# Experts' weights loaded in pairs of units, with the array laid out in order of use

## The chip, the cores and the metric

One core of a Trainium2 chip runs the whole kernel. The metric is the device time of one execution in microseconds, as the median of several runs. The profile is one further execution under the hardware profiler.

## The reference

One layer of a diffusion backbone over 1024 tokens of width 1024. A first part (modulated RMSNorm, one input projection, a long convolution and a neighbourhood attention, two branches merged by gates, an output projection) gives the residual stream `x`. The change concerns what follows, a mixture of experts with expert choice:

```python
def _ec_ffn(h, w_router, w_gate, w_up, w_down):
    cap = EC_CAPACITY * L // N_EXPERTS                        # 2 * 1024 / 16 = 128
    aff = jax.nn.softmax((h @ w_router).astype(jnp.float32), axis=-1)
    g, idx = lax.top_k(jnp.swapaxes(aff, 1, 2), cap)
...
    def expert(args):
        xe, wg, wu, wd = args
        return (jax.nn.silu(xe @ wg) * (xe @ wu)) @ wd
    y_e = lax.map(expert, (x_e, w_gate, w_up, w_down))
```

Each of 16 experts takes the 128 tokens with the highest affinity. Its three matrices are 1024 x 2816, 1024 x 2816 and 2816 x 1024 in float32. The results, weighted by the affinity, are added at the tokens' rows, and a gated residual and a last RMSNorm end the layer.

## The kernel before

The weights of all experts are arranged on the host (`units_laid_out`) as **units**: 128 partitions x 2048 floats, 1 MB, 8 KB per partition. An expert has 33 of them (`UNITS`): for each of six chunks `c` of the 2816 columns two units of gate and two of up, and for the chunk before it two of down; the last chunk is 256 wide and its gate and up share units ("both"). `STREAM` is the order in which units are used: expert by expert, except that the last unit of expert e, `CARRIED`, comes after the first two units of expert e+1. `PLACE` gives the place g of a unit in this order; there are N_ALL = 528.

The precision of a float32 product is had from three faster products: ACT copies a unit into a rounded high part `w_hi` (`split` on the scalar engine, L2702), DVE subtracts it from the raw unit for the low part `w_lo` (L2769), and PE multiplies high by high, low by high and high by low (L2657 for gate and up, L2647 for down): 12 matmuls of 512 columns for a unit. Ten units of expert 0 (`WHOLE`: places 0, 1, 4 to 7, 10 to 13) are not split; PE multiplies them as they are (L2623).

Three rings carry this. `raw` holds `RAW` = 8 units as they came; `w_hi` and `w_lo` hold `PARTS` = 6 each. SP loads unit g into slot g % 8 as soon as unit g-8 has been read for the last time, that is when its low part is ready, or when PE has used it if it is in `WHOLE`:

```python
for g in range(RAW, N_ALL):
    if g - RAW in WHOLE:
        sp.wait_ge(used, g - RAW + 1)
    else:
        sp.wait_ge(lo_ready, parts_until(g - RAW))
    sp.dma_start(raw[:, g % RAW], unit_source(a, g)).then_inc(raw_in[g % RAW], 16)
```

Each slot has its semaphore `raw_in[slot]`, which rises by 16 for each load. ACT's split of g waits for it and for `used` of g-6; DVE's for ACT's; PE waits for `lo_ready`. The first eight units are loaded one at a time by the stage before (`project_out`, L2028), while other transfers run.

The order on each engine is written out. ACT and DVE walk over g, split unit g and do what `STEPS` puts at g: silu of a gate chunk, the product with up (`moe_h`), the copy and low part of the transposed hidden chunk (`moe_ht_hi`, `moe_ht_lo`), the same for the tokens, the scaled output. In expert 0 DVE also finds the tokens of experts 1 to 15, in 16 rounds (`next_round`, L2779 to L2782) of which three come before the first unit and the others at g of `ROUNDS_AT` = 4, 5, 6, 7, 8, 10, 11, 12, 13, 14, 16, 17, 18. A down unit on PE waits for `h_parts`, which `moe_ht_lo` of its chunk raises: unit 8 for chunk 0, unit 14 for chunk 1. The low part of chunk 1 stands on DVE behind the split and the round of g = 17.

Of the kernel before, what the change touches and what calls it, by code (L numbers as in the profile page):

```python
# [1933 lines left out]
def project_out(nc, sems, a, keep, m_t, raw, raw_in, halves, gate_col, idx_col):  # L1934

    ident = keep["ident"]
    with ExitStack() as ctx:
# [56 lines left out]
        with nc.Block() as block:  # L1994

            @block.sync
            def _(sp):
                mod = a["mod_d"]
                x_t, acc_t, h2_t_d = (a[n].rearrange("(t p) d -> t p d", p=P) for n in ("x", "acc_d", "h2_d"))

                def load(t):
                    if t >= 2:
                        sp.wait_ge(x1_ready, t - 1)
                    sp.dma_start(x_in[:, t % 2], x_t[t]).then_inc(xt_in[t % 2], 16)

                def store(t):
                    sp.wait_ge(x1_ready, t + 1 + (t == LAST))
                    sp.dma_start(acc_t[t], x1[:, t % 2]).then_inc(stored[t % 2], 16)
                    sp.wait_ge(normed, t + 1)
                    sp.dma_start(h2_t_d[t], h2[:, t % 2]).then_inc(stored[t % 2], 16)  # L2010

                sp.dma_start(router[:], a["w_router"].rearrange("(k p) e -> p k e", p=P)).then_inc(cols_in, 16)
                for x, (src, at) in enumerate(((mod, 3 * D), (mod, 4 * D), (a["norm2_g"], 0))):
                    sp.dma_start(col_rows[x * KD:(x + 1) * KD], bass.AP(src.tensor, at, [[P, KD], [1, P]])).then_inc(cols_in, 16)
                for dst, at in ((g1_row, 2 * D), (shift_row, 3 * D), (scale_row, 4 * D)):
                    sp.dma_start(dst[:], bass.AP(mod.tensor, at, [[0, P], [1, D]])).then_inc(rows_in, 16)
                sp.dma_start(gain_row[:], bass.AP(a["norm2_g"].tensor, 0, [[0, P], [1, D]])).then_inc(rows_in, 16)
                sp.dma_start(tables[:], a["rank_tables"]).then_inc(rows_in, 16)
                load(0)
                load(1)  # L2020
                for t in range(TT):
                    if t == 1:
                        sp.wait_ge(keep["wo_lo"], KD)
                    if t == 6:
                        sp.wait_ge(m_split, TT)
                    units = {1: [0], 2: [1], 3: [2], 4: [3], 6: [4, 5, 6, 7]}.get(t, [])
                    for u in units:
                        sp.dma_start(raw[:, u], unit_source(a, u)).then_inc(raw_in[u], 16)  # L2028
                    store(t)
                    if t + 2 < TT:  # L2030
                        load(t + 2)
                for s in range(2):
                    sp.wait_ge(stored[s], 32 * TT // 2)
# [322 lines left out]
STREAM = []  # L2356
# [6 lines left out]
PLACE = {eu: g for g, eu in enumerate(STREAM)}  # L2363
RAW = 8
# [2 lines left out]
LAST_OF |= {(name, N_C - 1): LAST_OF["both", N_C - 1] for name in ("gate", "up")}  # L2367


def unit_source(a, g):  # L2370
    return a["w_moe"][STREAM[g]]


def units_laid_out(w_gate, w_up, w_down):

    e = w_gate.shape[0]
    by_k = {n: w.reshape(e, KD, P, FF) for n, w in (("gate", w_gate), ("up", w_up))}
    by_f = w_down.reshape(e, FF // P, P, D)
    out = np.empty((e, N_U, P, 2048), np.float32)
    for u, (name, c, q, parts) in enumerate(UNITS):  # L2380
        at, w = CHUNKS[c]
        if name == "down":
            f = at // P + 2 * q
            part = by_f[:, f:f + 2]
        elif name == "both":
            rows = slice(KD // parts * q, KD // parts * (q + 1))
            part = np.concatenate([by_k[n][:, rows, :, at:at + w] for n in ("gate", "up")], axis=3)
        else:
            rows = KD // parts
            part = by_k[name][:, rows * q:rows * (q + 1), :, at:at + w]  # L2390
        out[:, u] = part.transpose(0, 2, 1, 3).reshape(e, P, 2048)
    return out


def unit_view(slot, u):
# [5 lines left out]
def experts(nc, sems, a, keep, raw, raw_in, halves, gate_col, idx_col, out):  # L2401

    ident = keep["ident"]
    with ExitStack() as ctx:
# [3 lines left out]
        with ExitStack() as places:  # L2408
            n = Maker(nc, places, "moe_")
# [50 lines left out]
        def parts_until(g):  # L2460

            return g + 1 - sum(w <= g for w in WHOLE)
# [55 lines left out]
        with nc.Block() as block:  # L2518

            @block.sync  # L2520
            def _(sp):
                sp.dma_start(g2_row[:], bass.AP(a["mod_d"].tensor, 5 * D, [[0, P], [1, D]])).then_inc(g2_in, 16)
                for g in range(RAW, N_ALL):
                    if g - RAW in WHOLE:
                        sp.wait_ge(used, g - RAW + 1)
                    else:
                        sp.wait_ge(lo_ready, parts_until(g - RAW))
                    sp.dma_start(raw[:, g % RAW], unit_source(a, g)).then_inc(raw_in[g % RAW], 16)
                sp.wait_ge(keep["kept"], KEPT_NA)

            @block.gpsimd
# [57 lines left out]
            def _(pe):  # L2589
# [21 lines left out]
                def unit(e, u):  # L2611
                    name, c, q, parts = UNITS[u]
                    w = CHUNKS[c][1]
                    hi, lo = (unit_view(x[:, PLACE[e, u] % PARTS], u) for x in (w_hi, w_lo))
                    if PLACE[e, u] in WHOLE:
                        pe.wait_ge(raw_in[PLACE[e, u] % RAW], 16 * (PLACE[e, u] // RAW + 1))
                        source = unit_view(raw[:, PLACE[e, u] % RAW], u)
                        if c > 1 and q == 0:
                            pe.wait_ge(multiplied, N_C * e + c - 1)
                        ps = (ps_up if name == "up" else ps_gate)[:, c % 2]  # L2620
                        for r in range(KD // parts):
                            k = KD // parts * q + r
                            mm = pe.matmul(ps, xt_whole[:, k, :], source[:, r, :], start=(k == 0), stop=(k == KD - 1))  # L2623
                        mm.then_inc(used, 1)
                        return
                    pe.wait_ge(lo_ready, parts_until(PLACE[e, u]))
                    if name == "down":
                        if q == 0:
                            pe.wait_ge(h_parts, N_C * e + c + 1)
                        if q == 0 and c == 0 and e:  # L2630
                            pe.wait_ge(y_ready, e)
                        if (e, u) == (LAST_E, CARRIED):
                            for n in range(2):
                                cols = slice(n * 512, (n + 1) * 512)
                                for f in range(2):
                                    ht = [x[:, c % 2, f, :] for x in (ht_hi, ht_lo)]
                                    for x, (hp, wp) in enumerate(((ht[0], hi), (ht[0], lo), (ht[1], hi))):
                                        mm = pe.matmul(ps_y[:, cols], hp, wp[:, f, cols], start=False, stop=(f == 1 and x == 2))
                                mm.then_inc(used, 1)
                            return  # L2640
                        for r in range(2):
                            f = 2 * q + r
                            ht = [x[:, c % 2, f, :] for x in (ht_hi, ht_lo)]
                            first, last = c == 0 and f == 0, c == N_C - 1 and f == w // P - 1
                            for x, (hp, wp) in enumerate(((ht[0], hi), (ht[0], lo), (ht[1], hi))):
                                for n in range(2):
                                    mm = pe.matmul(ps_y[:, n * 512:(n + 1) * 512], hp, wp[:, r, n * 512:(n + 1) * 512],  # L2647
                                                   start=(first and x == 0), stop=(last and x == 2))
                    else:
                        ps = (ps_up if name == "up" else ps_gate)[:, c % 2]  # L2650
                        if q == 0 and N_C * e + c > 1:
                            pe.wait_ge(multiplied, N_C * e + c - 1)
                        rows = KD // parts
                        for r in range(rows):
                            k = rows * q + r
                            for x, (hp, wp) in enumerate(((xt_hi, hi), (xt_hi, lo), (xt_lo, hi))):
                                mm = pe.matmul(ps, hp[:, e % 2, k, :], wp[:, r, :], start=(k == 0 and x == 0),  # L2657
                                               stop=(k == KD - 1 and x == 2))
                    mm.then_inc(used, 1)
# [29 lines left out]
            def _(act):  # L2689
# [6 lines left out]
                def split(g):  # L2696
                    if g in WHOLE:
                        return
                    act.wait_ge(raw_in[g % RAW], 16 * (g // RAW + 1))
                    if g >= PARTS:  # L2700
                        act.wait_ge(used, g - PARTS + 1)
                    act.activation(w_hi[:, g % PARTS], raw[:, g % RAW], ACT.Copy).then_inc(hi_ready, 1)  # L2702
# [308 lines left out]
```

## Time and profile before

| | |
|---|---|
| median of 3 runs | 2612.39 us (2612.01 to 2615.18) |
| the profiled execution | 2610.21 us, its span 2608.4 us |
| mean granted clock of TensorE | 0.991 |
| PE busy | 2525.1 us (97%) |
| DVE busy | 2111.0 us (81%) |
| ACT busy | 1461.0 us (56%) |
| expert stage | from about 1080 us to the end |
| chain that ended last, by lines | PE L2657 gate 19%, L2647 down 18%, L2657 up 16% |
| moved by DMA | 798.95 MB, of which 528 loads of 1024 KB into `raw` |

The span is what the profiler saw from the first to the last instruction; 1.8 us of the execution's time lie around it. Busy times are unions over the engine's instructions. PE's matmuls overlap in the records, so that a busy PE is not one at its peak.

### The profile page before, as it was taken

Reading aid. Unit: us, or ns where it says so; the run is one execution under the profiler, and the core shown is the slowest. Engines: PE = TensorE matmul, PEld = TensorE weight load, DVE = VectorE, ACT = ScalarE, POOL = GpSimd, SP = SyncE. Lnnn points to the kernel's source line nnn. Section 1 sums busy time; section 2 is a strip of 40 time slices with the busy share of each in tenths; the row PEclk is TensorE's granted clock in tenths of the full one; section 3 lists DMA queues with packets and bytes.
Section 4 is the critical chain, followed back from the end, with each engine's and each line's share of the span. In section 5 each row is a group of like instructions: output and inputs, shape, how many; then the busy total and the mean of one; then the engine's idle time right before and its main releaser. Section 6 shows DMA issues by size and latency. Waiting matters only on the chain.

```text
span 2608.4 us, 31471 instructions
## 1 busy us (share of the span) xinstructions
PE 2525.1 (97%) x12268; PEld 2085.1 (80%) x12268; DVE 2111.0 (81%) x2106; ACT 1461.0 (56%) x1259; POOL 170.7 (7%) x181
## 2 busy tenths in 40 slices
PE   6999999999999999799999999999999999999997
PEld 3777889987877878568888888888888888888885
DVE  6775348678889666899988989989988998898997
ACT  4422237532121211357777777777777777777776
POOL 0011000011111000000000000000000000000002
PEclk9999999999999999899999999999999999999999
DMA  8798755665567634499999999999999999999996
GB/s 316 268 322 289 223 132 137 221 190 154 168 188 234 230 127 185 176 367 412 377 397 385 368 392 389 372 385 390 378 374 394 384 367 393 386 368 390 391 379 254
DMA packets 201173, 798.95 MB, mean 306 GB/s; under 512 B 18151, under 2 KB 67687, under 8 KB 131008
## 3 DMA queue, kind: packets, MB, share of 16 engines
q1 hardware_dynamic: 167236, 698.80, 70.8%
q0 software_dynamic: 32480, 96.50, 11.9%
q10 hardware_dynamic: 1310, 1.64, 0.3%
q8 instruction: 98, 1.61, 0.2%
q14 instruction: 49, 0.40, 0.0%
HBM read 722.67 MB, written 70.01 MB: 304 GB/s over the span
## 4 chain that ended last, share of the span: by engine, by line
PE 55%; DVE 2%; issue 0%; DMA 0%; ACT 0%; POOL 0%; DVEq 0%; ACTq 0%
PE moe_ps_gate L2657 19%; PE moe_ps_y L2647 18%; PE moe_ps_up L2657 16%; PE moe_ps_h L2608 1%; DVE moe_w_lo L2769 1%; PE moe_ps_x L2598 1%; DVE moe_where L2780 0%; DVE moe_rows L2782 0%; DVE moe_best L2779 0%; PE moe_ps_gate L2623 0%; DMA out<-raw 0%; ACT moe_w_hi L2702 0%; DVE raw L2878 0%; DVE moe_ht_lo L2839 0%; DVE moe_h L2834 0%
## 5 line engine op out<-in xcount | busy, mean ns | idle before, releaser
L2769 DVE TENSOR_TENSOR moe_w_lo<-raw,moe_w_hi 128x2048 fp32r<-128x2048 f32 x518 | 1184.8, 2291 | 142.6 <-ACT moe_w_hi L2702 138.8
L2702 ACT ACTIVATE moe_w_hi<-raw 128x2048 fp32r<-128x2048 f32 x518 | 994.7, 1920 | 390.0 <-PE moe_ps_gate L2657 145.1
L2657 PE MATMUL moe_ps_gate<-moe_w_hi,moe_xt_hi 128*128 128x512 f32 x744 | 294.0, 395 | 0.0
L2657 PE MATMUL moe_ps_gate<-moe_w_hi,moe_xt_lo 128*128 128x512 f32 x744 | 290.3, 390 | 0.0
L2657 PE MATMUL moe_ps_gate<-moe_w_lo,moe_xt_hi 128*128 128x512 f32 x744 | 289.7, 389 | 0.0
L2657 PE MATMUL moe_ps_up<-moe_w_hi,moe_xt_hi 128*128 128x512 f32 x624 | 249.3, 400 | 0.0
L2657 PE MATMUL moe_ps_up<-moe_w_hi,moe_xt_lo 128*128 128x512 f32 x624 | 243.5, 390 | 0.0
L2657 PE MATMUL moe_ps_up<-moe_w_lo,moe_xt_hi 128*128 128x512 f32 x624 | 242.8, 389 | 0.0
L2647 PE MATMUL moe_ps_y<-moe_w_hi,moe_ht_hi 128*128 128x512 f32 x700 | 216.0, 390 | 3.6 <-DVE moe_ht_lo L2839 3.6
L2647 PE MATMUL moe_ps_y<-moe_w_hi,moe_ht_lo 128*128 128x512 f32 x700 | 215.7, 389 | 0.0
L2647 PE MATMUL moe_ps_y<-moe_w_lo,moe_ht_hi 128*128 128x512 f32 x700 | 215.5, 389 | 0.0
L1517 PE MATMUL hyena_ps_g<-hyena_h_parts,hyena_g_parts 128*128 128x512 f32 x768 | 181.3, 393 | 4.8 <-DMA hyena_g_parts<-gw_d 2.9
L1517 PEld LDWEIGHTS hyena_ps_g<-hyena_h_parts,hyena_g_parts 128*128 128x128 f32 x768 | 143.0, 188 | 36.3 <-issue 4.7
L2657 PEld LDWEIGHTS moe_ps_gate<-moe_w_hi,moe_xt_lo 128*128 128x128 f32 x744 | 139.6, 188 | 29.7
L2657 PEld LDWEIGHTS moe_ps_gate<-moe_w_lo,moe_xt_hi 128*128 128x128 f32 x744 | 139.9, 188 | 27.8
L2657 PEld LDWEIGHTS moe_ps_gate<-moe_w_hi,moe_xt_hi 128*128 128x128 f32 x744 | 139.7, 188 | 27.6
L2647 PEld LDWEIGHTS moe_ps_y<-moe_w_hi,moe_ht_hi 128*128 128x128 f32 x700 | 131.0, 188 | 32.5 <-issue 3.4
L2647 PEld LDWEIGHTS moe_ps_y<-moe_w_lo,moe_ht_hi 128*128 128x128 f32 x700 | 131.4, 188 | 27.4
L2647 PEld LDWEIGHTS moe_ps_y<-moe_w_hi,moe_ht_lo 128*128 128x128 f32 x700 | 131.4, 188 | 27.4
L1646 DVE TENSOR_TENSOR hyena_spec<-hyena_spec 128x1024 f32<-128x1024 f32 (+2 forms) x120 | 139.5, 1218 | 15.0 <-ACT hyena_spec L1568 14.6
L2657 PEld LDWEIGHTS moe_ps_up<-moe_w_hi,moe_xt_lo 128*128 128x128 f32 x624 | 117.1, 188 | 25.3
L2657 PEld LDWEIGHTS moe_ps_up<-moe_w_lo,moe_xt_hi 128*128 128x128 f32 x624 | 117.5, 188 | 22.9 <-issue 0.2
(393 smaller groups left out, 3817.1 us busy)
## 6 DMA issues: line engine op xcount, KB each, us to landing
raw<-in_w_moe SPq DMA_DIRECT2D x528, 1024.0 KB, 7.2
hyena_g_parts<-gw_d POOLq DMA_DIRECT2D x64, 512.0 KB, 4.7
proj_w_mod<-in_w_mod SPq DMA_DIRECT2D x32, 512.0 KB, 6.8
gw_d<-proj_g_parts POOLq DMA_DIRECT2D x16, 1024.0 KB, 7.1
w_in<-in_w_in SPq DMA_DIRECT2D x12, 1024.0 KB, 8.7
attn_table<-in_na_table SPq DMA_DIRECT2D x16, 576.0 KB, 5.7
norm_w_mod<-in_w_mod SPq DMA_DIRECT2D x16, 512.0 KB, 10.7
proj_g_raw<-in_w_in SPq DMA_DIRECT2D x16, 512.0 KB, 9.9
```

The costliest lines, as they stand in the source:

```text
L1517: mm = pe.matmul(ps_g[:, n % 2, :], g_parts[:, g % G_SLOTS, w, k % G_K, :], h_parts[:, h, k, :], start=(k == 0 and y == 0), stop=(k == KD ...
L1646: dt.inc(dve.tensor_tensor(out, in0, in1, op))
L2598: mm = pe.transpose(x_turned(e, half)[:, k * P:(k + 1) * P], xe[:, at:at + P], ident[:])
L2608: mm = pe.transpose(ps_h[:, b * P:(b + 1) * P], h[:, c % 2, b * P:(b + 1) * P], ident[:])
L2647: mm = pe.matmul(ps_y[:, n * 512:(n + 1) * 512], hp, wp[:, r, n * 512:(n + 1) * 512], start=(first and x == 0), stop=(last and x == 2))
L2657: mm = pe.matmul(ps, hp[:, e % 2, k, :], wp[:, r, :], start=(k == 0 and x == 0), stop=(k == KD - 1 and x == 2))
L2702: act.activation(w_hi[:, g % PARTS], raw[:, g % RAW], ACT.Copy).then_inc(hi_ready, 1)
L2769: dve.tensor_tensor(w_lo[:, g % PARTS], raw[:, g % RAW], w_hi[:, g % PARTS].bitcast(F32), ALU.subtract).then_inc(lo_ready, 1)
```

## The change

The host lays the units out in the order of `STREAM`, one array of 528 units. SP loads them in pairs from place 8 on: one DMA brings units g and g+1 into two neighbouring slots, after both slots are free, and raises only the semaphore of the even slot. `landed` says which semaphore and value a unit waits for: its own below 8, that of its pair from 8 on. PE and ACT use it. The first eight units are loaded as before.

```diff
--- before.py
+++ after.py
@@ -2025,7 +2025,7 @@
                         sp.wait_ge(m_split, TT)
                     units = {1: [0], 2: [1], 3: [2], 4: [3], 6: [4, 5, 6, 7]}.get(t, [])
                     for u in units:
-                        sp.dma_start(raw[:, u], unit_source(a, u)).then_inc(raw_in[u], 16)
+                        sp.dma_start(raw[:, u:u + 1], unit_source(a, u)).then_inc(raw_in[u], 16)
                     store(t)
                     if t + 2 < TT:
                         load(t + 2)
@@ -2367,8 +2367,13 @@
 LAST_OF |= {(name, N_C - 1): LAST_OF["both", N_C - 1] for name in ("gate", "up")}
 
 
-def unit_source(a, g):
-    return a["w_moe"][STREAM[g]]
+def unit_source(a, g, units=1):
+    return a["w_moe"][g:g + units].rearrange("u p n -> p u n")
+
+
+def landed(raw_in, g):
+
+    return (raw_in[g % RAW], 16) if g < RAW else (raw_in[g % RAW // 2 * 2], 16 * (g // RAW + 1))
 
 
 def units_laid_out(w_gate, w_up, w_down):
@@ -2389,7 +2394,7 @@
             rows = KD // parts
             part = by_k[name][:, rows * q:rows * (q + 1), :, at:at + w]
         out[:, u] = part.transpose(0, 2, 1, 3).reshape(e, P, 2048)
-    return out
+    return out[tuple(np.array(STREAM).T)]
 
 
 def unit_view(slot, u):
@@ -2520,12 +2525,13 @@
             @block.sync
             def _(sp):
                 sp.dma_start(g2_row[:], bass.AP(a["mod_d"].tensor, 5 * D, [[0, P], [1, D]])).then_inc(g2_in, 16)
-                for g in range(RAW, N_ALL):
-                    if g - RAW in WHOLE:
-                        sp.wait_ge(used, g - RAW + 1)
-                    else:
-                        sp.wait_ge(lo_ready, parts_until(g - RAW))
-                    sp.dma_start(raw[:, g % RAW], unit_source(a, g)).then_inc(raw_in[g % RAW], 16)
+                for g in range(RAW, N_ALL, 2):
+                    for free in (g - RAW, g + 1 - RAW):
+                        if free in WHOLE:
+                            sp.wait_ge(used, free + 1)
+                        else:
+                            sp.wait_ge(lo_ready, parts_until(free))
+                    sp.dma_start(raw[:, g % RAW:g % RAW + 2], unit_source(a, g, 2)).then_inc(raw_in[g % RAW], 16)
                 sp.wait_ge(keep["kept"], KEPT_NA)
 
             @block.gpsimd
@@ -2613,7 +2619,7 @@
                     w = CHUNKS[c][1]
                     hi, lo = (unit_view(x[:, PLACE[e, u] % PARTS], u) for x in (w_hi, w_lo))
                     if PLACE[e, u] in WHOLE:
-                        pe.wait_ge(raw_in[PLACE[e, u] % RAW], 16 * (PLACE[e, u] // RAW + 1))
+                        pe.wait_ge(*landed(raw_in, PLACE[e, u]))
                         source = unit_view(raw[:, PLACE[e, u] % RAW], u)
                         if c > 1 and q == 0:
                             pe.wait_ge(multiplied, N_C * e + c - 1)
@@ -2696,7 +2702,7 @@
                 def split(g):
                     if g in WHOLE:
                         return
-                    act.wait_ge(raw_in[g % RAW], 16 * (g // RAW + 1))
+                    act.wait_ge(*landed(raw_in, g))
                     if g >= PARTS:
                         act.wait_ge(used, g - PARTS + 1)
                     act.activation(w_hi[:, g % PARTS], raw[:, g % RAW], ACT.Copy).then_inc(hi_ready, 1)
```

What SP issues in the expert stage, with what each waits for, at the start of the ring. `moe_g_row` is a row of the modulation, `used_units` the semaphore `used`, `m_lo_ready` is `lo_ready`. The rows with - are of before, those with + of the change; x506 says that 506 such rows follow one another.

```order
-L2522 DMA moe_g_row<-mod_d 128x1024
-L2528 DMA raw<-in_w_moe 128x2048 [waits used_units] x2
-L2528 DMA raw<-in_w_moe 128x2048 [waits m_lo_ready] x2
-L2528 DMA raw<-in_w_moe 128x2048 [waits used_units] x4
-L2528 DMA raw<-in_w_moe 128x2048 [waits m_lo_ready] x2
-L2528 DMA raw<-in_w_moe 128x2048 [waits used_units] x4
-L2528 DMA raw<-in_w_moe 128x2048 [waits m_lo_ready] x506
+L2534 DMA raw<-in_w_moe 128x2x2048 [waits used_units]
+L2534 DMA raw<-in_w_moe 128x2x2048 [waits m_lo_ready]
+L2534 DMA raw<-in_w_moe 128x2x2048 [waits used_units] x2
+L2534 DMA raw<-in_w_moe 128x2x2048 [waits m_lo_ready]
+L2534 DMA raw<-in_w_moe 128x2x2048 [waits used_units] x2
+L2534 DMA raw<-in_w_moe 128x2x2048 [waits m_lo_ready] x253
```

The six groups of before are units 8 and 9, 10 and 11, 12 to 15, 16 and 17, 18 to 21, and the rest; each group of two has become one DMA, and it waits for the second of the two slots.

What ACT does in the same place, from the copy of unit 8 to the copy of unit 17, before:

```order
431 L2702 ACTIVATE moe_w_hi<-raw 128x2048 [waits used_units,raw_in0]
432 L2702 ACTIVATE moe_w_hi<-raw 128x2048 [waits used_units,raw_in1]
433 L2727 ACTIVATE moe_ht_hi<-moe_ps_h 128x512 [waits turned_h]
434 L2723 ACTIVATE moe_sl<-moe_ps_gate 128x512 [waits used_units]
435 L2702 ACTIVATE moe_w_hi<-raw 128x2048 [waits used_units,raw_in6]
436 L2702 ACTIVATE moe_w_hi<-raw 128x2048 [waits used_units,raw_in7]
437 L2702 ACTIVATE moe_w_hi<-raw 128x2048 [waits used_units,raw_in0]
438 L2702 ACTIVATE moe_w_hi<-raw 128x2048 [waits used_units,raw_in1]
```

and with the change:

```order
431 L2708 ACTIVATE moe_w_hi<-raw 128x2048 [waits used_units,raw_in0] x2
432 L2733 ACTIVATE moe_ht_hi<-moe_ps_h 128x512 [waits turned_h]
433 L2729 ACTIVATE moe_sl<-moe_ps_gate 128x512 [waits used_units]
434 L2708 ACTIVATE moe_w_hi<-raw 128x2048 [waits used_units,raw_in6] x2
435 L2708 ACTIVATE moe_w_hi<-raw 128x2048 [waits used_units,raw_in0] x2
```

No instruction of ACT has moved; both units of a pair wait for the even slot's semaphore. Lines below 2370 keep their numbers, those of the expert stage are 6 higher.

## Rows read from the trace of the kernel before

**Rows 1.** Stretches: length, busy of PE, PEld, DVE, ACT, POOL; clock, DMA share, GB/s.
```profile
1103.70:1115.30 11.60, 11.17 (x30) 4.79 (x28) 11.39 (x19) 1.09 (x2) 0.00 (x0) 1.00 0.79 285
1120.40:1136.40 16.00, 14.86 (x40) 6.69 (x38) 15.78 (x21) 9.67 (x7) 0.00 (x0) 1.00 0.79 292
...
1160.00:2570.00 1410.00, 1410.00 (x6437) 1167.12 (x6436) 1270.29 (x738) 1057.48 (x720) 78.19 (x41) 1.00 0.99 385
```

**Rows 2.** Waits from 1145 to 2570 us: total us, times, longest.
```profile
ACT moe_w_hi L2702 <- PE moe_ps_gate L2657: 145.1, 182, 1.4
DVE moe_w_lo L2769 <- ACT moe_w_hi L2702: 136.3, 356, 1.0
ACT moe_w_hi L2702 <- PE moe_ps_y L2647: 121.7, 166, 1.1
ACT moe_w_hi L2702 <- PE moe_ps_up L2657: 90.0, 150, 0.8
```

**Rows 3.** DVE in order of time: start, us, what, [idle before <- releaser].
```profile
1103.00 0.66 DVE L2782 MATCH_REPLACE8 moe_rows<-moe_best,moe_rows 32x512 f32<-32x512 f32 x1
1103.70 2.29 DVE L2769 TENSOR_TENSOR moe_w_lo<-raw,moe_w_hi 128x2048 fp32r<-128x2048 f32 x1
...
1120.42 2.29 DVE L2769 TENSOR_TENSOR moe_w_lo<-raw,moe_w_hi 128x2048 fp32r<-128x2048 f32 x1 [0.26 <-ACT moe_w_hi L2702]
...
1124.77 2.29 DVE L2769 TENSOR_TENSOR moe_w_lo<-raw,moe_w_hi 128x2048 fp32r<-128x2048 f32 x1
...
1135.69 0.69 DVE L2839 TENSOR_TENSOR moe_ht_lo<-moe_ps_h,moe_ht_hi 128x512 fp32r<-128x512 f32 x1
1136.29 2.28 DVE L2769 TENSOR_TENSOR moe_w_lo<-raw,moe_w_hi 128x2048 fp32r<-128x2048 f32 x1
```

**Rows 4.** PE in order of time: starts of units 8, 14 and 18, end of unit 13.
```profile
1115.40 0.47 PE L2647 MATMUL moe_ps_y<-moe_w_hi,moe_ht_hi 128*128 128x512 f32 x1 [0.53 <-DVE moe_ht_lo L2839]
...
1134.24 1.02 PE L2623 MATMUL moe_ps_up<-raw,moe_whole 128*128 128x512 f32 x2
1136.52 0.47 PE L2647 MATMUL moe_ps_y<-moe_w_hi,moe_ht_hi 128*128 128x512 f32 x1 [1.26 <-DVE moe_ht_lo L2839]
...
1147.88 0.48 PE L2657 MATMUL moe_ps_up<-moe_w_hi,moe_xt_hi 128*128 128x512 f32 x1
```

**Rows 5.** ACT in order of time: the copies of units 8 and 14.
```profile
1098.08 1.92 ACT L2702 ACTIVATE moe_w_hi<-raw 128x2048 fp32r<-128x2048 f32 x1 [2.22 <-PE moe_ps_up L2657]
...
1118.47 1.92 ACT L2702 ACTIVATE moe_w_hi<-raw 128x2048 fp32r<-128x2048 f32 x1 [9.34 <-PE moe_ps_y L2647]
```

**Rows 6.** SP's DMA issues: unit 9; units 15 to 17, and their landing.
```profile
1095.24 0.33 SPq L2528 DMA_DIRECT2D raw<-in_w_moe  x1
...
1114.90 1.28 SPq L2528 DMA_DIRECT2D raw<-in_w_moe  x3
...
L2528 SPq DMA_DIRECT2D raw<-in_w_moe x3: 328/430/432, 1114.9 to 1115.8; - x3
...
DMA to landing us min/median/max: 4.8/6.9/8.9
```

**Rows 7.** DMA issues: count, KB each, median us to landing.
```profile
raw<-in_w_moe SPq DMA_DIRECT2D x528, 1024.0 KB, 7.2
...
hq_d<-h_hi SPq DMA_DIRECT2D x2, 2048.0 KB, 7.0
```

**Rows 8.** Stretches with pauses of PE, columns as in rows 1.
```profile
959.40:961.50 2.10, 0.00 (x0) 0.00 (x0) 2.03 (x4) 0.00 (x0) 0.00 (x0) 1.00 0.13 53
961.70:965.00 3.30, 3.30 (x8) 2.65 (x9) 2.18 (x2) 1.05 (x2) 0.00 (x0) 0.50 0.08 32
965.10:968.50 3.40, 3.40 (x16) 2.82 (x15) 1.83 (x7) 1.49 (x2) 0.00 (x0) 1.00 0.27 111
590.00:597.20 7.20, 2.72 (x15) 2.10 (x13) 7.20 (x8) 0.97 (x2) 0.00 (x0) 1.00 0.37 147
```

**Rows 9.** Units 301 (issue), 300 (copy), loads 1201.8 to 2500.0, unit 518 (issue, landing, copy).
```profile
1916.71 0.33 SPq L2528 DMA_DIRECT2D raw<-in_w_moe  x1
...
1932.84 1.93 ACT L2702 ACTIVATE moe_w_hi<-raw 128x2048 fp32r<-128x2048 f32 x1 [0.53 <-PE moe_ps_y L2647]
...
DMA to landing us min/median/max: 4.7/7.1/12.7
...
L2528 SPq DMA_DIRECT2D raw<-in_w_moe x1: 327/327/327, 2530.6 to 2530.6; - x1
...
DMA to landing us min/median/max: 13.1/13.1/13.1
...
2548.98 1.91 ACT L2702 ACTIVATE moe_w_hi<-raw 128x2048 fp32r<-128x2048 f32 x1
```

## The prediction

> **What bounds the kernel now.** I read the stretches of the expert stage first, to see which engine is never idle. From 1160 to 2570 us PE is busy 1410.00 of 1410.00 us [rows 1]: for 54% of the span nothing but PE's own work counts. Next the waits of that stage: ACT's copies wait 498 times for PE and DVE's splits for ACT; no wait of PE, ACT or DVE for a DMA is in the list [rows 2]. The weights therefore always lie there before they are asked for, although 16 DMA engines are busy 0.99 of the time [rows 1]. So in the long stage a faster or slower transfer can only eat or add cover.
>
> The start of the stage is different. There units 0, 1, 4 to 7 and 10 to 13 go to PE unsplit, DVE is between its splits also choosing tokens (rounds of max, max_index, match_replace), and the ring has just begun to turn. DVE runs from one operation into the next there: before unit 8's split at 1103.70 us stands the round that ends at 1103.66, and PE waits for DVE twice: 0.53 us before unit 8 and 1.26 us before unit 14, both for ht_lo of DVE [rows 3, 4]. Unit 14's split even waited 0.26 us for ACT's copy, which began at 1118.47 [rows 3, 5]. This is the place where a later landing is paid.
>
> **The price of a transfer.** One unit that is loaded alone lands 4.8 us after its issue, and three that are issued within 0.9 us (at +0, +0.37 and +0.85) land 4.8, 6.9 and 8.9 us after their own issues [rows 6], which is 4.8, 7.3 and 9.8 after the first: 2.5 us for each further MB. A pair issued alone should land after 4.8 + 2.5 = 7.3 us, and both halves at once, since one semaphore speaks for both. The row nearest to it is a store of 2048 KB, 7.0 us; loads of the ring have a median of 7.2 because they queue [rows 7].
>
> The Trainium skill ("DMA: Bandwidth & Descriptors", anatomy of one DMA) fits 2.0 us plus bytes over 436 GB/s for a transfer issued by GpSimd: 4.4 us for 1 MB and 6.8 us for 2 MB, an estimate; by it the sum below would be 0.5 us less. Its 4.4 is 0.4 under the 4.8 of rows 6, so I stay with the rows.
>
> **The change, step by step.**
> 1. *Layout in order of use.* It moves one unit in 33. Pieces stay 8 KB per partition. Nothing, either way, beside the queue's rate of rows 1.
> 2. *Half the DMA issues on SP.* 260 instead of 520, 0.33 us each [rows 6]: SP has nothing else to do in this stage. 0.
> 3. *Pair 8/9.* It waits for units 0 and 1; the second of these releases it at 1095.24, where unit 9 is issued now [rows 6]. It lands at 1095.2 + 7.3 = 1102.5. ACT copies unit 8 from 1102.6 to 1104.5 (1.92 us; now 1098.08) [rows 5], and DVE's split goes from 1103.70 to 1104.5: +0.8 us. All behind it on DVE moves along, ht_lo and PE's unit 8 too: PE's pause grows from 0.5 to 1.3 us.
> 4. *Pair 14/15.* It waits until unit 7 is used, 1114.90 [rows 6], and that is not moved by step 3 (units 4 to 7 need only what landed long ago). It lands at 1122.2; copy to 1124.1; split at 1124.2 instead of 1120.42 [rows 3]: +3.8 us. The 0.8 of step 3 is inside it, not on top: the later one decides. From there DVE is busy 15.78 of 16.00 us up to ht_lo at 1135.69 [rows 1, 3], so all 3.8 us arrive: ht_lo at 1139.5, PE's unit 14 at 1140.3 instead of 1136.52 [rows 4].
> 5. *Pair 16/17* follows in the queue and lands at 1122.2 + 5.0 = 1127.2; copied by 1129.2, wanted by DVE at 1130.9 (2.3 us after unit 15's split began at 1124.77 + 3.8 [rows 3]). Covered by 1.7 us. Pairs 18/19 to 26/27 come out in the same way with 1 to 2 us before DVE wants them, and DVE itself is far ahead of PE by then: unit 18 is split from 1136.29 to 1138.57 and multiplied from 1147.88 [rows 3, 4], 9.3 us. If this cover went, each us too late would be paid once.
> 6. *PE's longer pause and its clock.* PE ends unit 13 at 1135.26, then 1136.1, and waits to 1140.3: 4.2 us instead of 1.26 [rows 4]. In this trace a pause of 2.1 us (959.4 to 961.5) was followed by 3.3 us at a granted clock of 0.50 (1.2 instead of 2.4 GHz), with 8 matmuls where the next 3.4 us at 1.00 hold 16 [rows 8]; that loses 1.7 us. Against it, 4.5 us of idleness in two pieces (2.72 busy of 7.20) left the clock at 1.00 [rows 8]. Bounds 0 and 1.7 us; I take 1.5, nearer the single pause, part of the low stretch falling into the pause itself. PE is the bound from there, so nothing hides it.
> 7. *The long stage.* A pair is issued one split later than its first unit is now (2.7 us) and that unit lands up to 2.5 us later. Example: units 300/301 would be issued at 1916.71; even at the longest landing seen there, 12.7 us, the copy at 1932.84 is not late [rows 9]. 0.
> 8. *The tail.* The accumulated rows are read beside the ring. The tightest unit, 518, is issued at 2530.6 and lands 13.1 us later, 2543.7; ACT copies it at 2548.98 [rows 9]. With a queue that full the pair lands when its second half does now, about 2.5 us later: 2546.2, still 2.8 us early. 0.
>
> Sum: 3.8 + 1.5 = **+5.3 us**. The profiled execution took 2610.21 us, the median of the runs is 2612.39; against the first that is 2615.5, against the second **2617.7**.
>
> **Rivals.** What a measurement of this kernel can tell from no change is about 0.2%, 5.2 us; the forecast lies on that edge.
> - *The clock holds* (the piecewise pause of rows 8 speaks for it, the 2.1 us pause against it): +3.8, 2616.2. This is the rival that ends on the other side, not slower; it decides at whether the clock after unit 14 is 1.00. Chance 0.24.
> - *2 MB lands sooner than 7.3 us*, for example 5.5 because a lone MB leaves room in the queue: then split 14 is at +2.0 and the clock stays: 2614.4. The store of 7.0 and the even 2.5 us of rows 6 speak against it. Chance 0.10.
> - *2 MB lands later*, 8.3 or more: the longer DMA instruction has twice the descriptors to make before the last one goes, and one request of 2 MB cannot start its second half early. Each us adds one in step 4 and lengthens the pause: +6.3 to +8, 2619 to 2621. The rows hold no load of 2 MB that was alone, so nothing excludes it. Chance 0.20.
> - *The queue gets slower in the long stage*: PE needs 1 MB each 2.7 us and the queue gives one each 2.5; if pairs took over 2.8, PE would wait in all 16 experts, tens of us. Same pieces, same rate: chance 0.04.
> - *Faster.* The Trainium skill ("Perfetto Trace Analysis", DMA Optimizations) says that larger DMAs saturate HBM better. By rows of this kernel, all that better arrival can remove is PE's two pauses, 1.8 us [rows 4], which is not measurable; a real gain needs a shorter matmul, 1 ns on each of about 6200. Chance 0.05. [...]
> - *The change does not do what it says*: the order of SP shows one DMA of 128x2x2048 for two of 128x2048, so this is set aside.
>
> **How the numbers follow.** Forecast 0.37 (with a clock term of 1.1 to 1.7 us it spans 4.9 to 5.5, across the edge of 5.2), rivals as above. Same: 0.24 + 0.10 + 0.10 from the forecast = 0.44. Slower: 0.20 + 0.04 + 0.27 = 0.51, the forecast's larger half with it since every small delay left out would add. Faster 0.05. The range runs from the early landing (2614) to the late one with a low clock (2623); outside are the starved queue and the gain.
>
> **What the profile would show.** Pairs alone landing after 7.3 us; unit 8's split at 1104.5; unit 14's copy near 1122.3, its split at 1124.2, with ACT now waiting for a DMA; PE's pause before unit 14 4.2 us and the clock 0.50 after it; PE without a gap from there to 2570 + 5; no wait for a DMA in the long stage. I am wrong if unit 14's split is not late, if PE waits anywhere after it, or if the matmul's step changes.

## The result, and the profile after

| | before | after |
|---|---|---|
| median | 2612.34 us (8 runs, 2607.36 to 2615.18) | 2620.15 us (8 runs, 2614.92 to 2623.9) |
| the profiled execution, its span | 2610.21, 2608.4 us | 2619.6, 2617.8 us |
| mean granted clock of TensorE | 0.991 | 0.988 |

The ratio of the times is 1.0029, 95% interval 1.0020 to 1.0037: 7.6 us slower, where 5.3 was forecast (the forecast was 2617.7 us, its range 2614 to 2623). The cost lies at the start of the expert stage and a little of it at its end, none between.

What SP's DMA issues of pairs 8/9 and 14/15 say, each in its own stretch, and those of the long stage (first and last start; minimum, median and longest us to landing), to hold against [rows 6, 9]:

```profile
L2534 SPq DMA_DIRECT2D raw<-in_w_moe x1: 384/384/384, 1097.0 to 1097.0; - x1
DMA to landing us min/median/max: 7.4/7.4/7.4
...
L2534 SPq DMA_DIRECT2D raw<-in_w_moe x1: 367/367/367, 1116.7 to 1116.7; - x1
DMA to landing us min/median/max: 7.5/7.5/7.5
...
L2534 SPq DMA_DIRECT2D raw<-in_w_moe x230: 367/368/368, 1201.3 to 2496.5; - x115
DMA to landing us min/median/max: 7.4/9.8/14.3
```

A pair alone lands after 7.4 to 7.5 us; 7.3 was the estimate. ACT, DVE and PE in order of time at the same places, to hold against [rows 5, 3, 4]: ACT's copies of units 8 and 14; DVE's split of unit 14 and ht_lo of chunk 1; PE's first matmul of the stage and its starts of units 8 and 14.

```profile
1104.44 1.91 ACT L2708 ACTIVATE moe_w_hi<-raw 128x2048 fp32r<-128x2048 f32 x1 [6.85 <-DMA raw<-in_w_moe]
1124.19 1.91 ACT L2708 ACTIVATE moe_w_hi<-raw 128x2048 fp32r<-128x2048 f32 x1 [13.36 <-DMA raw<-in_w_moe]
...
1126.13 2.29 DVE L2775 TENSOR_TENSOR moe_w_lo<-raw,moe_w_hi 128x2048 fp32r<-128x2048 f32 x1 [3.23 <-ACT moe_w_hi L2708]
1141.40 0.69 DVE L2845 TENSOR_TENSOR moe_ht_lo<-moe_ps_h,moe_ht_hi 128x512 fp32r<-128x512 f32 x1
...
1089.82 0.70 PE L2629 MATMUL moe_ps_gate<-raw,moe_whole 128*128 128x512 f32 x1 [0.25 <-ACT moe_whole L2718]
1118.14 0.47 PE L2653 MATMUL moe_ps_y<-moe_w_hi,moe_ht_hi 128*128 128x512 f32 x1 [1.56 <-DVE moe_ht_lo L2845]
1142.24 0.77 PE L2653 MATMUL moe_ps_y<-moe_w_hi,moe_ht_hi 128*128 128x512 f32 x1 [4.24 <-DVE moe_ht_lo L2845]
```

ACT, which waited only for PE before, now waits for the DMA; DVE waits 3.23 us for ACT where it waited 0.26; PE waits 4.24 us before unit 14 where it waited 1.26. Then the stretches (columns as in [rows 1]): the end of the pause, units 14 and 15 after it, an equal stretch behind them, and the long stage.

```profile
1140.70:1142.20 1.50, 0.00 (x0) 0.00 (x0) 1.47 (x5) 1.14 (x1) 0.00 (x0) 0.50 1.02 431
1142.30:1147.40 5.10, 5.10 (x12) 4.04 (x13) 5.03 (x8) 0.00 (x0) 0.00 (x0) 0.50 1.01 427
1147.50:1152.60 5.10, 5.10 (x24) 4.23 (x23) 3.95 (x4) 3.84 (x2) 0.00 (x0) 1.00 1.01 424
1160.00:2570.00 1410.00, 1410.00 (x6436) 1166.89 (x6434) 1269.51 (x733) 1056.31 (x717) 74.34 (x36) 1.00 0.99 384
```

The clock is at its lower level (0.50, 1.2 GHz) for the end of the pause and 5.1 us of work: 12 matmuls where the next 5.1 us hold 24. In the long stage PE is busy 1410.00 of 1410.00 us, as in [rows 1]; DVE and ACT wait as in [rows 2], and again for no DMA. It is closer than that sounds. I call the time from a load's landing to the start of ACT's copy its cover: for the even units from 28 to 502 its median was 11.3 us before and is 5.9 us now, and the least was 3.7 us and is 0.2 us, for pair 378/379. That pair's issue with its landing, and the copy, which still waits for PE and not for the load:

```profile
L2534 SPq DMA_DIRECT2D raw<-in_w_moe x1: 368/368/368, 2146.8 to 2146.8; - x1
DMA to landing us min/median/max: 14.3/14.3/14.3
...
2161.32 1.93 ACT L2708 ACTIVATE moe_w_hi<-raw 128x2048 fp32r<-128x2048 f32 x1 [0.80 <-PE moe_ps_y L2653]
```

At the tail ACT waits for a tile of the residual stream, read from `acc_d` by GpSimd beside the ring, and a gap of PE grows. ACT's wait and PE's gap, then the median landing of the five such reads:

```profile
2579.21 1.06 ACT L2742 ACTIVATE moe_discarded<-raw 128x1024 bf16<-128x1024 f32 x1 [1.23 <-DMA raw<-acc_d]
...
2588.53 0.44 PE L2614 MATMUL moe_ps_h<-identity,moe_h 128*128 128x128 f32 x2 [1.44 <-DVE moe_h L2840]
...
raw<-acc_d POOLq DMA_DIRECT2D x5, 512.0 KB, 9.5
```

The same gap and the same row of before:

```profile
2579.11 0.66 PE L2608 MATMUL moe_ps_h<-identity,moe_h 128*128 128x128 f32 x4 [0.38 <-DVE moe_h L2834]
...
raw<-acc_d POOLq DMA_DIRECT2D x5, 512.0 KB, 7.0
```

**Where the time went.** I count from the first matmul of the stage, since the code before it is the same: it starts at 1088.08 us before and at 1089.82 after, and between 1088.1 and 1091.7 in the eleven profiles of the experiments. These 1.7 us between the two profiled executions are no work of the change.

| from the stage's first matmul, us | before | after | difference |
|---|---|---|---|
| PE starts unit 8 | 27.32 | 28.32 | +1.00 |
| PE starts unit 14 | 48.45 | 52.42 | +3.97 |
| PE starts unit 16 | 54.00 | 60.40 | +6.40 |
| DVE splits unit 520 | 1468.98 | 1475.51 | +6.53 |
| end | 1520.33 | 1527.98 | +7.65 |

Late start of unit 14 4.0, low clock in units 14 and 15 2.4, long stage 0.1, tail 1.1: 7.6 us, which is what the ratio of the runs gives.

### The profile page after: what moved, and what is told of

Read it like the earlier page. It is cut to its first block, busy times and chain, and to the rows that moved or that the text cites. A ratio compares the mean times of both kernels' runs of the same rounds, so it can differ in the third digit from the quotient of the medians.

```text
span 2617.8 us, 31471 instructions
## 1 busy us (share of the span) xinstructions
PE 2531.2 (97%) x12268; PEld 2088.9 (80%) x12268; DVE 2111.6 (81%) x2106; ACT 1460.1 (56%) x1259; POOL 170.5 (7%) x181
## 4 chain that ended last, share of the span: by engine, by line
PE 56%; DVE 1%; DMA 1%; issue 0%; ACT 0%; POOL 0%; DVEq 0%; SPq 0%
PE moe_ps_gate L2663 19%; PE moe_ps_y L2653 18%; PE moe_ps_up L2663 16%; PE moe_ps_h L2614 1%; DVE moe_w_lo L2775 1%; PE moe_ps_gate L2629 1%; PE moe_ps_x L2604 1%; DMA raw<-in_w_moe 0%; PE moe_ps_up L2629 0%; DMA out<-raw 0%; PE moe_ps_x L2671 0%; DVE raw L2884 0%; DVE moe_where L2786 0%; DVE moe_rows L2788 0%; ACT moe_w_hi L2708 0%
```

## The experiments

All but the fillers are made from the changed kernel with one function that sets how many units a load brings; semaphores and waits follow from it:

```diff
+def load_size(g):
+    return 1
...
-                for g in range(RAW, N_ALL, 2):
-                    for free in (g - RAW, g + 1 - RAW):
+                for g, n in LOADS:
+                    for free in range(g - RAW, g - RAW + n):
```

| kernel | ratio, 95% interval | unit 14 | unit 16 | unit 20 | split 520 | end |
|---|---|---|---|---|---|---|
| before | | 48.45 | 54.00 | 65.38 | 1468.98 | 1520.33 |
| the change | 1.0029, 1.0020 to 1.0037 | 52.42 | 60.40 | 71.77 | 1475.51 | 1527.98 |
| e_layout | 0.9999, 0.9990 to 1.0008 | 48.60 | 54.16 | 65.53 | 1469.34 | 1520.79 |
| e_middle | 1.0004, 0.9995 to 1.0013 | 48.42 | 53.98 | 65.36 | 1469.14 | 1520.59 |
| e_tail | 1.0000, 0.9991 to 1.0009 | 48.57 | 54.12 | 65.49 | 1469.25 | 1521.83 |
| e_early | 1.0022, 1.0013 to 1.0031 | 52.27 | 60.51 | 71.88 | 1475.69 | 1528.81 |
| e_early_again | 1.0023, 1.0014 to 1.0033 | 52.36 | 60.56 | 71.93 | 1475.72 | 1527.27 |
| e_only | 1.0026, 1.0015 to 1.0036 | 52.36 | 60.48 | 71.86 | 1475.59 | 1527.02 |
| e_one | 1.0016, 1.0006 to 1.0025 | 49.52 | 55.05 | 68.08 | 1472.22 | 1524.59 |
| e_late | 1.0013, 1.0004 to 1.0022 | 49.60 | 55.13 | 66.50 | 1470.22 | 1524.81 |
| e_filled | 1.0035, 1.0021 to 1.0048 | 54.71 | 60.26 | 71.64 | 1477.22 | 1529.64 |
| e_fill34 | 1.0024, 1.0015 to 1.0033 | 52.53 | 58.09 | 69.45 | 1473.74 | 1526.13 |
| e_four | 1.091, 1.089 to 1.093 | 71.81 | 78.70 | 90.07 | 1708.5 | 1763.69 |

Times are starts on PE (of the split on DVE), in us from the stage's first matmul, each from one profile.

### Which loads cost: the layout, the start, the middle, the tail

`e_layout` has `return 1`. 

> Only the array's new order; every unit is loaded alone. Theory (the time is lost where a pair lands later than one unit did: 3.8 us before unit 14, 2.5 us of low clock after it, 1.1 us at the tail): the layout costs nothing, total within 1 us of before, PE's pause before unit 14 back at 1.3 us, clock 1.00 after it. Rival (the new order of the array makes the loads slower): loads alone land later than 4.8 us, and part of the 7.5 us stays.

Measured: a ratio of 0.9999, unit 14 at 48.60, no pause beyond those of before. The array's order costs nothing and gains nothing that these runs can tell.

`e_early`:

```diff
+    return 2 if g < 28 else 1
```

> Pairs only for units 8 to 27, single loads from 28 on. Theory: the pause of 4.2 us before unit 14 and the low clock behind it stay, the 1.1 us at the tail go: 6 to 6.5 us slower than before. Rival (pairs cost a little in every expert): most of the 7.5 us goes, under 3 us remain.

Measured: 1.0022; unit 14 +3.8, unit 16 +6.5, 0.2 us more by unit 520. Ten pairs carry all of the early cost, the low clock included. The end of this profile is +8.5, more than the change's: its tail took 1.8 us more than before, which comes back below.

`e_middle`:

```diff
+    return 2 if 28 <= g < 504 else 1
```

> Pairs only for units 28 to 503, 476 of the 528. Theory: 0, within 1 us of before, PE without a gap through the long stage though the cover of a copy shrinks to 0.2 us at the least. Rival (pairs cost a little in every expert): nearly all of the 7.5 us is here.

Measured: 1.0004, unit 520 +0.2 us. Two stretches of it, the issues with their landing and the long stage:

```profile
DMA to landing us min/median/max: 6.7/9.8/14.2
...
1160.00:2490.00 1330.00, 1330.00 (x6076) 1100.70 (x6075) 1198.16 (x691) 992.63 (x671) 67.71 (x29) 1.00 0.99 384
```

The pairs land up to 14.2 us after their issue, and PE is never idle. Each unit is there later than a single load would bring it, and that costs nothing here. It uses up cover, though: the least in this profile is 0.7 us, for pair 446/447. What is shown is that pairs fit into the long stage of this ring, not that there is room left.

`e_tail`:

```diff
+    return 2 if g >= 504 else 1
```

> Pairs only for units 504 to 527. Theory: +1.1 us, ACT waits about 1.2 us for a row tile read from acc that queues behind a pair, and PE has a second gap of 1.4 us in the last expert. Rival (the tail's gap comes from the stage's later state, not from the pairs): 0 and no such wait.

Measured: the interval reaches from 0.9991 to 1.0009 and does not show 1.1 us. The profile does: from unit 520 to the end 52.58 us, before 51.35.

```profile
2574.15 1.06 ACT L2757 ACTIVATE moe_discarded<-raw 128x1024 bf16<-128x1024 f32 x1 [1.34 <-DMA raw<-acc_d]
...
raw<-acc_d POOLq DMA_DIRECT2D x5, 512.0 KB, 9.5
```

Other profiles say the same. Where the last loads are single (before, e_layout, e_middle, e_only) the reads landed after 7.0 to 7.1 us, ACT did not wait for them, and from unit 520 to the end it took 51.4 to 51.5 us. Where they come in pairs (the change, e_tail, e_one, e_fill34, e_filled) the reads landed after 8.9 to 9.5 us, in e_filled after 8.0, ACT waited 1.2 to 1.3 us, and it took 52.4 to 52.6 us. e_late, whose single loads come bunched, had 9.5 and a wait of 1.7. One case did not fit: e_early, single at the end, had 8.1, a wait of 1.9 and 53.1 us. So I ran it again.

> The kernel with pairs only for units 8 to 27 once more. In its first profile the last scatter into acc took 12.1 us where before it took 9.5, the reads of acc landed 8.1 us after their issue instead of 7.0, and PE had a second gap in the last expert though the ring there is single. Theory (that was the scatter of this one execution; the tail's gap belongs to pairs near the end): scatter near 9.5, reads at 7.0, no wait of ACT for acc, second gap 0.4 us. Rival (the early pairs reach the tail by some path): gap above 1 us again.

Measured: reads at 7.1, wait 0.3, second gap 0.6, from unit 520 to the end 51.6 us, but the last scatter took 11.7 us again, which I had called an accident. The early pairs do not bring the tail's cost as a rule; why the scatter is longer in this kernel than in e_only (9.8) is open. The step from the later read to the gap of PE is read from the profiles and was not tried by itself, and the runs alone do not show the tail's 1.1 us.

### One pair

`e_only` pairs units 14 and 15 alone:

```diff
+    return 2 if g == 14 else 1
```

> One pair alone, units 14 and 15; the other 518 loads bring one unit each. Theory: this one transfer is the whole early loss: it lands 7.3 us after its issue at unit 7's end, unit 14 starts 3.8 us later counted from the first matmul of the stage, PE's pause is 5.0 us, the clock falls, 6 to 6.5 us in all. Rival (the first pair 8/9, or the ring's state over several pairs, makes the loss): under 2 us.

Measured: 1.0026. ACT's copy of unit 14 and PE's start of it:

```profile
1122.38 1.91 ACT L2723 ACTIVATE moe_w_hi<-raw 128x2048 fp32r<-128x2048 f32 x1 [13.26 <-DMA raw<-in_w_moe]
...
1140.43 0.77 PE L2668 MATMUL moe_ps_y<-moe_w_hi,moe_ht_hi 128*128 128x512 f32 x1 [5.11 <-DVE moe_ht_lo L2860]
```

One transfer of 260 is the early cost: unit 14 is +3.9 and unit 16 +6.5, as with all pairs. Pair 8/9 costs nothing beside it; its 1.0 us only turns part of the pause into an earlier one (5.11 here, 1.56 and 4.24 in the change).

`e_one` is its complement:

```diff
+    return 1 if g in (14, 15) else 2
```

> The change with units 14 and 15 loaded alone, all others in pairs. Theory: unit 14 starts only 0.8 us late (pair 8/9). A table of the dependences with this trace's durations gives 1.7 us more at unit 20, because ht_lo of chunk 2 stands on DVE behind the splits of the pairs 20/21 and 22/23, which land later too; 2.5 us in all, clock at 1.00 unless that pause is long. Rival (removing the pair frees everything, since DVE is 9 us ahead of PE at unit 18, as the prediction held): 0.8 us in all.

Measured: unit 14 +1.07, unit 20 +2.70, the clock high. PE's start of unit 20:

```profile
1157.42 0.47 PE L2668 MATMUL moe_ps_y<-moe_w_hi,moe_ht_hi 128*128 128x512 f32 x1 [1.50 <-DVE moe_ht_lo L2860]
```

The rival, which was my own step 5, is wrong: behind the first tight place stands a second one. Unit 20 is a down unit; it needs ht_lo of chunk 2, which DVE does only after the split of unit 23. On the way there DVE waits for copies of three pairs, of which my table had only the last two: its splits of unit 18, of units 20 and 21, and of 22 and 23 in this run:

```profile
1139.76 2.29 DVE L2790 TENSOR_TENSOR moe_w_lo<-raw,moe_w_hi 128x2048 fp32r<-128x2048 f32 x1 [1.04 <-ACT moe_w_hi L2723]
1147.18 4.49 DVE L2790 TENSOR_TENSOR moe_w_lo<-raw,moe_w_hi 128x2048 fp32r<-128x2048 f32 x2 [0.43 <-ACT moe_w_hi L2723]
1152.18 4.49 DVE L2790 TENSOR_TENSOR moe_w_lo<-raw,moe_w_hi 128x2048 fp32r<-128x2048 f32 x2 [0.51 <-ACT moe_w_hi L2723]
```

In the change this is covered, because DVE and PE are later than that by then.

### Later issue, or joint landing

`e_late` loads single units but keeps the wait for both slots:

```diff
-                    for free in range(g - RAW, g - RAW + n):
+                    for free in range(g - RAW, g // 2 * 2 + 2 - RAW):
```

> No pairs: each unit is loaded alone, but the first of two neighbours waits until both slots are free, as in the change. This keeps the later issue and takes away the joint landing. Theory: unit 14 is issued where the pair was and lands after 4.8 us instead of 7.4: its split is 1.3 us late instead of 3.8, PE's pause about 2.5 us; 1.3 us in all, up to 3 with a low clock. Rival (the wait for the second slot is the whole cost): 3.8 us before unit 14 as in the change.

```profile
1139.88 0.47 PE L2668 MATMUL moe_ps_y<-moe_w_hi,moe_ht_hi 128*128 128x512 f32 x1 [2.52 <-DVE moe_ht_lo L2860]
```

Measured: unit 14 +1.15, the clock stays high, unit 520 +1.24. So of the 4.0 us before unit 14 1.2 come from the later issue (unit 14 is issued 3.5 us later, most of which its cover takes up) and 2.8 from the landing of both units at once. The end is +4.5, though: the tail took 3.2 us more, with a low clock of 3.4 us while PE was on units 523 and 524. The ratio, 1.0013, holds both.

### What the low clock costs

`e_filled` is the change with work for PE in its pause:

```diff
+                    if (e, u) == (0, 14):
+                        for n in range(FILL):
+                            pe.transpose(ps_x[:, n % 4 * P:(n % 4 + 1) * P], ident[:], ident[:])
                     unit(e, u)
```

> The change, with 60 transposes of the identity on PE (into a free part of PSUM, nothing reads them) between units 13 and 14, so that PE is busy in its pause while it still waits for the same event. They are extra work and leave nothing out. Theory: the granted clock stays 1.00 from there on and 2.5 us come back, about 5 us slower than before. Rival (the low clock is not caused by the pause, or costs nothing because DVE bounds there): no gain over the change, 7.5 us.

```profile
1139.10:1145.50 6.40, 6.40 (x60) 6.40 (x59) 6.33 (x9) 3.72 (x2) 0.00 (x0) 1.00 0.82 300
```

Measured: the clock stayed at 1.00, and the gain was spent: 60 transposes took 6.7 us, unit 14 began at 54.71, and by unit 16 all was as in the change. So far this miss says only that the filler was too long. Its profile ends 1.7 us after the change's, for another reason: near the end its pairs landed up to 17.2 us after their issue (14.9 in the change), ACT waited for pairs 514/515 and 516/517, and PE paused before unit 515. ACT's waits from 2490 to 2600 us and PE's pause:

```profile
ACT moe_w_hi L2712 <- DMA raw<-in_w_moe: 3.4, 2, 1.8
...
2565.01 0.70 PE L2654 MATMUL moe_ps_y<-moe_w_hi,moe_ht_hi 128*128 128x512 f32 x2 [1.46 <-DVE moe_ht_lo L2849]
```

In the change the cover of pair 516/517 was 0.5 us and that of 518/519 0.7 us (e_one and e_fill34: none and 0.7), where before units 516 and 518 had 8.1 and 5.3. Why the loads landed later in e_filled is open, but with pairs such an execution can lose time at the ring's end too. `e_fill34` sets FILL = 34.

> The same filler with 34 transposes instead of 60. The first filler kept the clock at 1.00 but took 6.7 us for a pause of 4.2 (0.112 us for each transpose), so that unit 14 began 2.3 us late by its own fault; 34 take 3.8 us and end inside the pause. Theory: clock 1.00 from there on, unit 14 where the change has it (52.4 us after the stage's first matmul), units 14 and 15 take 5.55 us instead of 7.98, so 2.4 us come back: about 5 us slower than before. Rival (the low clock's price is illusory, something behind it bounds): unit 20 begins 71.8 us after the first matmul as in the change.

```profile
1141.00:1143.00 2.00, 1.51 (x15) 1.30 (x13) 1.97 (x5) 1.85 (x2) 0.00 (x0) 1.00 0.96 406
1143.10:1148.10 5.00, 5.00 (x23) 4.10 (x24) 4.93 (x8) 1.85 (x1) 0.00 (x0) 1.00 1.01 428
```

Measured: unit 14 at 52.53 as in the change, unit 16 at 58.09 instead of 60.40, unit 20 at 69.45 instead of 71.77. Work in the pause, and nothing else, was added, and the clock stayed up: the pause causes the low clock, and the low clock costs 2.3 us at this place. At the end 1.9 us of them are left (1526.13 instead of 1527.98); where the rest went was not followed up. The runs' ratio, 1.0024, does not separate it from 1.0029.

### Four units in one transfer

`e_four` has `return 4`. 

> Four units, 4 MB, in one transfer from unit 8 on: the suspected cost doubled. It frees the ring only every fourth unit and should land 4.8 + 7.5 = 12.3 us after its issue. Theory (issue later plus joint landing, against about 15 us between the freeing of a slot's neighbour and the copy): a table of the dependences gives unit 8 6 us late, unit 14 21 us, and now also a loss in the long stage where the cover is gone, about 0.1 us for each unit: 80 to 150 us in all, with waits of ACT for raw<-in_w_moe in every expert. Rival (only the start is sensitive, a queue 0.99 busy keeps PE fed whatever the size): 20 to 30 us, all before unit 28.

Measured: 1.091, 238 us, more than the 80 to 150 of the theory. Its waits from 1145 us on, of which the list before has no wait for a load, and a stretch of the long stage:

```profile
ACT moe_w_hi L2723 <- DMA raw<-in_w_moe: 427.9, 113, 17.4
DVE moe_w_lo L2790 <- ACT moe_w_hi L2723: 387.6, 213, 14.4
...
1300.00:2700.00 1400.00, 1280.93 (x5566) 1038.33 (x5565) 1081.69 (x627) 888.55 (x615) 60.81 (x26) 0.96 0.85 333
```

With pairs the long stage still covers everything; with fours ACT waits for 115 of the 130 loads, and the DMA engines, 0.99 busy before, are at 0.85. That fits a ring of which half must be empty before the next transfer begins; no run here takes that wait away by itself. The table of dependences had neither the gathers and scatters beside the ring nor the clock, now 0.96 in the mean; how the missing 90 us divide among these was not tried.

No kernel here beats before: e_layout, e_middle and e_tail are the same within their intervals.

## Why the prediction was right, and which of its sizes were off

- **Bound and place.** That the long stage would cover the pairs and the start would not: right, shown by e_middle (238 pairs, 0) and e_only (one pair, all of the early cost).
- **Step 1, layout.** 0, measured 0 (ratio 0.9999). Step 2, fewer issues, was not measured by itself; e_middle bounds it with step 7.
- **Step 3, pair 8/9.** +0.8, measured +1.0, and inside step 4 as said.
- **Step 4, pair 14/15.** +3.8, measured +3.97. The landing is 7.5 us instead of 7.3; the rest of the working stands, the sequence of DVE from the split to ht_lo included.
- **Step 5, cover behind it.** The size was right for the change and the reason was not. The 9.3 us between the split of unit 18 and its use is not the cover of the pairs behind: ht_lo of chunk 2 is, and e_one lost 1.5 us of PE's time there once the first pause was gone. I had looked at the units' own use and not at what DVE does after their splits. The 1 to 2 us that I gave the pairs behind 16/17 before DVE wants them held only because DVE was 4.0 us late: in e_one, with DVE 1.1 us late, it stood idle 1.04 us for pair 18/19.
- **Step 6, pause and clock.** The pause of 4.2 us was right (4.24). The clock term was mis-sized: 1.5 forecast, within 0 and 1.7; measured 2.4, with e_fill34 as the check (2.3). I had taken the low stretch of [rows 8], 3.3 us, as the longest; here it was 6.8 us, 5.1 of them in work. The trace of before would have given a wider bound. It has a single pause of 4.5 us, nearer to 4.2 than any in [rows 8], with 3.3 us at 0.50 behind it, and another low stretch of 6.7 us with 5.40 us of work, by which the upper bound is 2.7 us (half of 5.40, an estimate) and not 1.7:

```profile
24.90:29.40 4.50, 0.06 (x2) 0.09 (x4) 3.23 (x5) 4.39 (x8) 0.00 (x0) 1.00 1.06 370
29.80:33.10 3.30, 3.30 (x10) 0.53 (x8) 2.88 (x9) 3.26 (x4) 0.00 (x0) 0.50 1.06 377
360.90:367.60 6.70, 5.40 (x25) 5.43 (x26) 3.74 (x10) 4.04 (x6) 0.00 (x0) 0.50 0.92 266
```

- **Step 7, long stage.** 0, measured 0.1 us. But units 300/301 were not the tightest place: their cover is 5.6 us in the change, that of 378/379 0.2 us. That nothing was lost there is in part luck.
- **Step 8, tail.** This step failed: 0 forecast, 1.1 measured. It looked at the ring's own units. They were in time in the change, but by 0.7 us for unit 518, not by 2.8, and in e_filled they were not. It did not ask what the 2 MB that are issued just before do to the reads of `acc_d` that GpSimd puts beside the ring.

5.3 and 7.6 differ by 2.3: 0.2 from step 4, 0.9 from the clock, 1.1 from the tail, 0.1 from the long stage. Of the rivals, the held clock, the early landing and the gain fell in the profile of the change, and the slower queue with e_middle. The rival with 8.3 us or more to land gave the right size of time (+6.3 to +8) for a wrong reason, since the pairs landed after 7.4 to 7.5. The forecast's own span, 4.9 to 5.5, was missed; that 2620.15 lies in the range is owed to the room that was left for that rival. And one of the signs of being wrong did come: PE waits 1.44 us in the tail, where it waited 0.38.

## What to carry to other kernels

A larger transfer through a ring costs latency twice, once because it waits for more free slots and once because its first part is only known to be there with its last; here these were 1.2 and 2.8 us. In this kernel it was free where the ring had that much cover and paid where it had not. So work out the least cover of a stage and not one example's, and look for the tightest place (a ring that has just begun to turn, a stage's tail with other reads beside it) before choosing one size for all loads. And ask what an engine does after the late operation, not only who uses its result.

## What the runs showed of the hardware that I had not expected

- A pause of PE of 4.2 us brought 6.8 us at the lower clock, of which the first part lay in the pause. A pause of 2.5 us (e_late) and one of 1.5 us (e_one) at the same stage left it at the higher level, while the 2.1 us pause of [rows 8] did not: the length of the pause alone does not tell. Nor is the low stretch of one pause fixed: that of the 4.5 us pause at 24.9 us was 3.4 us long in the profile of before and 6.8 us in that of the change, where it began in the pause.
- Transposes of the identity kept the clock up: with 34 of them in the pause, 3.8 us of work, it stayed at 1.00 (e_fill34).
- 2 MB alone land 2.7 us after 1 MB alone (7.5 to 4.8), near the 2.5 us for each further MB of [rows 6]; 4 MB alone, the first load of e_four, landed after 12.4 us. The DMA engines were 0.99 busy in the long stage with loads of 1 MB and of 2 MB. The Trainium skill ("DMA: Bandwidth & Descriptors", anatomy of one DMA) gives 6.8 us for 2 MB on the GpSimd path, an estimate from its fit; here, issued by SP, the trace shows 7.4 to 7.5.
- Reads of 512 KB from another queue landed 1 to 2.5 us later (8.0 to 9.5 instead of 7.0 to 7.1) when the ring beside them loaded 2 MB at a time.
